# Where the split weights and the moving rows of a two-layer block lie in SBUF: one spacing for all slots, one place for all rows

## The chip, the cores and the metric

One Trainium2 chip, one core of it, fp32 in and out. The metric is the device time of one launch in microseconds (us), the median of several runs. Five engines run side by side: TensorE (PE; its weight loads are a row of their own, PEld), VectorE (DVE), ScalarE (ACT), GpSimd (POOL) and SyncE (SP).

## The reference

256 tokens of width 1024 go through two layers. Each layer is, with one shared shape of step `x = x + gate * f(modulate(rms_norm(x)))`:

```python
for l in range(2):
    mod = silu(c) @ w_ada[l] + b_ada[l]                      # 9 vectors of 1024
    x = x + 0.5 * g1 * swiglu(h1, w_ff_in[l, 0], w_ff_out[l, 0])    # 1024 -> 2 x 2816 -> 1024
    x = x + g2 * token_mix(h2, ...)                          # window attention, RG-LRU, gated linear attention
    x = x + 0.5 * g3 * swiglu(h3, w_ff_in[l, 1], w_ff_out[l, 1])

def token_mix(h, ...):
    proj = h @ w_in                                          # 1024 -> 6416
    ys = [attention(...), rg_lru(...), gla(...)]             # three branches of 1024
    merged = sum_b sigmoid(h @ w_gate_b) * (ys[b] @ w_branch_b)
    return merged @ w_out
```

Nearly all of the arithmetic is in products of the 256 tokens with fp32 weights that are read once.

## The kernel before

**Slabs.** All weights are cut into slabs of 128 partitions x 2048 fp32, 8192 bytes in each partition: eight blocks `cc` of 128 input rows by 256 output columns, or, for the output product of a feed-forward half (`slab_rows`), two blocks of 128 rows by 1024 columns. There are 120 slabs to a layer, numbered `p` in the order in which TensorE uses them. SyncE loads slab `p` into `raw` slot `p % 4`. ScalarE copies it, rounded to fp32r, into `w_hi` slot `p % 3` (line 964), and VectorE puts the rest, `raw - w_hi`, into `w_lo` slot `p % 3` (line 1438). The activations are split in the same way (`h_hi`, `h_lo` and so on).

**A product.** For a slab, TensorE runs 48 matmuls of 128 x 128 weights and 256 moving columns (`slab_tile`, line 490). They come in threes: weights `w_hi` with rows `hi`, `w_hi` with rows `lo`, `w_lo` with rows `hi`. While one matmul streams its moving rows, the weights of the next are loaded:

```python
for q, (a, b) in enumerate(((w[0], hi), (w[0], lo), (w[1], hi))):
    last = mm(outs, a, b[:, cc, :], ...)
```

214 of the 240 slabs go through line 490. The others: lines 514 and 520 (first slab after a norm), 534 (in chunks, as pieces arrive), 620 (the lead of a norm, 258 columns), 680 (16 columns) and 837 (the values of the linear attention, where rows of `h` are the weights and the slab moves).

**What moves.** `h_hi`/`h_lo` (8 rows of 256 floats) for the input, gate and output projections. In a feed-forward half, block `j` of the hidden layer lies in `hid_hi`/`hid_lo` for even `j` and in the first two rows of `xm_hi`/`xm_lo` for odd `j`. The branch products of the token mix read `y_hi`/`y_lo`, which are views of the same `xm_hi`/`xm_lo`. The rows of `xm` are 258 floats apart, since the lead of a norm multiplies 256 tokens and a doubled shift column.

**Order in a feed-forward half.** It is written out by hand: gate slab of `j + 1`, output slab of `j`, up slab of `j + 1`, and so on. With three slots the output slabs (`down`) nearly all fall into slot 0, and the up and gate slabs into slots 1 and 2. So six slabs repeat: even output (slot 0), up (slot 1), gate (slot 2), odd output (slot 0), up (slot 1), gate (slot 2).

**Where the tiles lie.** Tiles are taken one behind the other in the order of the `sb(...)` calls. Counted from the start of `raw`, in bytes of a partition: `w_hi` at 32768, its slots 8256 apart (2048 + 16 floats); `w_lo` at 57536, also 8256 apart; `h_hi` 100736, `h_lo` 108928; `xm_hi` 117120, `xm_lo` 125376, rows 1032 apart; `hid_hi` 133632, `hid_lo` 135680.

Of the kernel before, what the change touches and what calls it, by code (L numbers as in the profile page):

```python
# [8 lines left out]
F32R = mybir.dt.float32r  # L9
# [8 lines left out]
T = 256  # L18
C = D // P
# [17 lines left out]
SPLIT = 3  # L37
# [67 lines left out]
def build(nc, x, c, w_ada, b_ada, norm_g, w_ff_in, w_ff_out, w_in, qk_norm_g, attn_sinks, rel_bias,  # L105
# [3 lines left out]
    with ctx:  # L109
        def sb(name, shape, dt=F32):  # L110
            return ctx.enter_context(nc.sbuf_tensor(name, [P] + shape, dt))
# [3 lines left out]


        raw = sb("raw", [RAW, 2048])
        w_hi = sb("w_hi", [SPLIT, 2048 + 16], F32R)[:, :, 0:2048]
        w_lo = sb("w_lo", [SPLIT, 2048 + 16], F32R)[:, :, 0:2048]
        rgw = sb("rgw", [2, 2, P])  # L120

        xT = sb("xT", [C, T])
        hf = sb("hf", [C, T])
        h_hi, h_lo = sb("h_hi", [C, T], F32R), sb("h_lo", [C, T], F32R)
        xm_hi, xm_lo = sb("xm_hi", [C, T + 2], F32R), sb("xm_lo", [C, T + 2], F32R)
        y_hi, y_lo = xm_hi[:, :, 0:T], xm_lo[:, :, 0:T]
        hid_hi, hid_lo = sb("hid_hi", [2, T], F32R), sb("hid_lo", [2, T], F32R)
        hid_h = (hid_hi[:, :, :], y_hi[:, 0:2, :])
        hid_l = (hid_lo[:, :, :], y_lo[:, 0:2, :])
        merged = hf  # L130


# [1763 lines left out]
```

## Time and profile before

| | |
|---|---|
| three runs | 1554.15, 1557.41, 1557.48 us; median 1557.41 |
| profiled execution | 1556.63 us, its span in the profile 1554.9 us |
| TensorE matmuls / weight loads busy | 1530.3 us / 1486.8 us |
| VectorE busy | 1133.2 us |
| ScalarE busy | 801.3 us |
| DMA | 333.52 MB, mean 214 GB/s |
| mean granted TensorE clock | 0.993 of full |

The span is the time from the first to the last instruction of the program. Matmuls are pipelined: the profile gives each some 280 ns although the next one starts after about 118 ns, so what a matmul costs is read from start to start, or from a row of the chain that puts many matmuls of one line together, and not from the mean of one.

### The profile page before, as it was taken

Reading aid. Unit: us, or ns where it says so; the run is one execution under the profiler, and the core shown is the slowest. Engines: PE = TensorE matmul, PEld = TensorE weight load, DVE = VectorE, ACT = ScalarE, POOL = GpSimd, SP = SyncE. Lnnn points to the kernel's source line nnn. Section 1 sums busy time; section 2 is a strip of 40 time slices with the busy share of each in tenths; the row PEclk is TensorE's granted clock in tenths of the full one; section 3 lists DMA queues with packets and bytes.
Section 4 is the critical chain, followed back from the end, with each engine's and each line's share of the span. In section 5 each row is a group of like instructions: output and inputs, shape, how many; then the busy total and the mean of one; then the engine's idle time right before and its main releaser. Section 6 shows DMA issues by size and latency. Waiting matters only on the chain.

```text
span 1554.9 us, 29266 instructions
## 1 busy us (share of the span) xinstructions
PE 1530.3 (98%) x12591; PEld 1486.8 (96%) x12591; DVE 1133.2 (73%) x1533; ACT 801.3 (52%) x970; POOL 25.2 (2%) x29
## 2 busy tenths in 40 slices
PE   7999999999999999999999999999999999999998
PEld 6999999999999999999999999999999899999998
DVE  4597777898556998776877768769865588977444
ACT  3444337888446346433464334677855544463342
POOL 0000000000100000000000000000001000000000
PEclk8899999999999999999999999999999999999999
DMA  9889855554456886778658785555454599675451
GB/s 338 291 246 282 280 170 163 151 158 140 144 163 214 301 305 210 260 265 284 208 202 284 259 295 168 147 166 149 138 161 145 171 310 330 217 256 198 164 192 52
DMA packets 284001, 333.52 MB, mean 214 GB/s; under 512 B 13084, under 2 KB 235200, under 8 KB 283872
## 3 DMA queue, kind: packets, MB, share of 16 engines
q1 hardware_dynamic: 276112, 327.40, 64.1%
q10 hardware_dynamic: 7760, 4.26, 1.1%
q8 instruction: 99, 1.62, 0.4%
q14 instruction: 30, 0.25, 0.1%
HBM read 330.23 MB, written 1.38 MB: 213 GB/s over the span
## 4 chain that ended last, share of the span: by engine, by line
PE 84%; DVE 10%; ACT 4%; issue 1%; DMA 0%; SPq 0%; DVEq 0%; ACTq 0%
PE ps L490 71%; DVE w_lo L1438 3%; PE ps L837 3%; DVE scratch L1335 1%; ACT w_hi L964 1%; PE ps L752 1%; PE ps L552 1%; DVE hf L1482 1%; DVE h_lo L1487 1%; PE ps L620 1%; PE ps L698 1%; DVE xT L1502 1%; PE ps L553 1%; PE ps L799 1%; PE ps L514 1%
## 5 line engine op out<-in xcount | busy, mean ns | idle before, releaser
L490 PE MATMUL ps<-h_hi,w_hi 128*128 128x256 f32 x2336 | 659.9, 282 | 0.8 <-DVE w_lo L1438 0.8
L490 PE MATMUL ps<-h_lo,w_hi 128*128 128x256 f32 x2336 | 653.2, 280 | 0.0
L490 PE MATMUL ps<-h_hi,w_lo 128*128 128x256 f32 x2336 | 651.4, 279 | 0.0
L1438 DVE TENSOR_TENSOR w_lo<-raw,w_hi 128x2048 fp32r<-128x2048 f32 x237 | 541.1, 2285 | 120.7 <-ACT w_hi L964 120.7
L964 ACT ACTIVATE w_hi<-raw 128x2048 fp32r<-128x2048 f32 x237 | 452.6, 1913 | 207.8 <-PE ps L490 203.1
L490 PEld LDWEIGHTS ps<-h_hi,w_hi 128*128 128x128 f32 x2336 | 438.3, 188 | 8.9 <-issue 7.1
L490 PEld LDWEIGHTS ps<-h_lo,w_hi 128*128 128x128 f32 x2336 | 439.8, 188 | 0.5 <-issue 0.5
L490 PEld LDWEIGHTS ps<-h_hi,w_lo 128*128 128x128 f32 x2336 | 439.8, 188 | 0.0
L490 PE MATMUL ps<-xm_hi,w_hi 128*128 128x256 f32 x704 | 199.8, 284 | 0.0
L490 PE MATMUL ps<-xm_hi,w_lo 128*128 128x256 f32 x704 | 198.7, 282 | 0.0
L490 PE MATMUL ps<-xm_lo,w_hi 128*128 128x256 f32 x704 | 197.9, 281 | 0.0
L1335 DVE SCALAR_TENSOR_TENSOR scratch<-eyr,cond,scratch 128x512 f32<-128x512 f32 x240 | 180.3, 751 | 10.5 <-DMA eyr<-in_w_ada_dram 1.7
L1551 DVE TENSOR_TENSOR t512b<-t512a,ps 128x512 f32<-128x512 f32 x41 | 28.2, 687 | 144.5 <-issue 92.9
L490 PEld LDWEIGHTS ps<-xm_hi,w_lo 128*128 128x128 f32 x704 | 133.1, 189 | 0.0
L490 PEld LDWEIGHTS ps<-xm_lo,w_hi 128*128 128x128 f32 x704 | 133.1, 189 | 0.0
L490 PEld LDWEIGHTS ps<-xm_hi,w_hi 128*128 128x128 f32 x704 | 132.9, 189 | 0.0
L490 PE MATMUL ps<-hid_hi,w_hi 128*128 128x256 f32 x384 | 109.1, 284 | 1.4 <-DVE hid_lo L1555 1.3
L490 PE MATMUL ps<-hid_lo,w_hi 128*128 128x256 f32 x384 | 108.1, 282 | 0.0
L490 PE MATMUL ps<-hid_hi,w_lo 128*128 128x256 f32 x384 | 107.1, 279 | 0.0
L490 PEld LDWEIGHTS ps<-hid_hi,w_hi 128*128 128x128 f32 x384 | 72.1, 188 | 2.0 <-DVE w_lo L1438 1.6
L490 PEld LDWEIGHTS ps<-hid_hi,w_lo 128*128 128x128 f32 x384 | 73.0, 190 | 0.0
L490 PEld LDWEIGHTS ps<-hid_lo,w_hi 128*128 128x128 f32 x384 | 72.2, 188 | 0.1
(269 smaller groups left out, 1762.8 us busy)
## 6 DMA issues: line engine op xcount, KB each, us to landing
raw<-in_w_ff_in_dram SPq DMA_DIRECT2D x176, 512.0 KB, 4.8
eyr<-in_w_ada_dram SPq DMA_DIRECT2D x144, 512.0 KB, 6.9
raw<-in_w_in_dram SPq DMA_DIRECT2D x100, 512.0 KB, 4.7
raw<-in_w_ff_out_dram SPq DMA_DIRECT2D x88, 512.0 KB, 4.8
raw<-in_w_gate_dram SPq DMA_DIRECT2D x48, 512.0 KB, 4.6
raw<-in_w_branch_dram SPq DMA_DIRECT2D x48, 512.0 KB, 4.6
raw<-in_w_out_dram SPq DMA_DIRECT2D x16, 512.0 KB, 5.3
rgw<-in_rg_w_dram ACTq DMA_DIRECT2D x16, 128.0 KB, 2.2
```

Of the source, the lines that this page charges most:

```text
L490: last = mm(outs, a, b[:, cc, :], start=clear and cc == 0 and q == 0, stop=cc == n - 1 and q == 2, skip_group_check=True)
L514: mm(ps[:, bank, t * T:(t + 1) * T], w_of[b][:, cc, t * P:(t + 1) * P], h_hi[:, cc, :], start=cc == 0 and b == 0 and t == 0, stop=False, s ...
L552: mm(to, ada_raw(2 * b + 1)[:, cc, cols], cond[:, 4 + cc:5 + cc], start=cc == 0, stop=False)
L553: last = mm(to, acc[:, cols], ones[:, 0:1], start=not direct, stop=True)
L620: last = mm(ps[:, first_bank + t, 0:T + 2], a, b[:, cc, :], start=cc == 0 and q == 0, stop=cc == C - 1 and q == 2, skip_group_check=True)
L698: last = nc.tensor.transpose(ps[:, 4 + hh, b * P:(b + 1) * P], pr[:, hh, b * P:(b + 1) * P], ident[:, :])
L752: last = mm(ps[:, 2 - g, t * T:(t + 1) * T], rgw[:, g, t, :], xc[:, t, :], start=True, stop=True)
L837: last = mm(ps[:, 1, m * T:(m + 1) * T], a, b, start=cc == 0 and q == 0, stop=cc == C - 1 and q == 2)
L964: f(w_hi[:, p % SPLIT, :], raw[:, p % RAW, :], ACT.Copy).then_inc(hi_ready, 1)
L1335: ins = stt(acc, w[:, cc, :], by, acc, ALU.mult, ALU.add)
L1438: tt(w_lo[:, p % SPLIT, :], raw[:, p % RAW, :], w_hi[:, p % SPLIT, :].bitcast(F32), ALU.subtract).then_inc(lo_ready, 1)
L1551: tt(t512b[:, :], t512a[:, :], ps[:, 5, :], ALU.mult).then_inc(hid_made, 1)
```

## The change

The split weights lose the pad of 16 floats behind each slot, so that slots lie exactly 8192 bytes apart. A pad of 192 bytes is put between `w_hi` and `w_lo`, and one of 128 bytes ahead of `h_hi`. `xm_hi` and `xm_lo` become two halves of one flat tile `xm`; the branch rows `y_hi`, `y_lo` become a view of it of their own, with rows 1024 bytes apart (not 1032) and `y_lo` 8192 bytes behind `y_hi`. The odd hidden block still lies in the first two rows of `xm_hi`/`xm_lo`, 1032 bytes apart, and `hid_hi`/`hid_lo` move ahead of `xm`. No instruction is added or removed.

```diff
-        w_hi = sb("w_hi", [SPLIT, 2048 + 16], F32R)[:, :, 0:2048]
-        w_lo = sb("w_lo", [SPLIT, 2048 + 16], F32R)[:, :, 0:2048]
+        w_hi = sb("w_hi", [SPLIT, 2048], F32R)
+        sb("place_low", [48])
+        w_lo = sb("w_lo", [SPLIT, 2048], F32R)
         rgw = sb("rgw", [2, 2, P])
 
         xT = sb("xT", [C, T])
         hf = sb("hf", [C, T])
+        sb("place_h", [32])
         h_hi, h_lo = sb("h_hi", [C, T], F32R), sb("h_lo", [C, T], F32R)
-        xm_hi, xm_lo = sb("xm_hi", [C, T + 2], F32R), sb("xm_lo", [C, T + 2], F32R)
-        y_hi, y_lo = xm_hi[:, :, 0:T], xm_lo[:, :, 0:T]
         hid_hi, hid_lo = sb("hid_hi", [2, T], F32R), sb("hid_lo", [2, T], F32R)
-        hid_h = (hid_hi[:, :, :], y_hi[:, 0:2, :])
-        hid_l = (hid_lo[:, :, :], y_lo[:, 0:2, :])
+        xm = sb("xm", [2 * C * (T + 2)], F32R)
+        xm_hi, xm_lo = (xm[:, b * C * (T + 2):(b + 1) * C * (T + 2)].rearrange("p (c t) -> p c t", c=C) for b in range(2))
+        y_hi, y_lo = (xm[:, b * C * T:(b + 1) * C * T].rearrange("p (c t) -> p c t", c=C) for b in range(2))
+        hid_h = (hid_hi[:, :, :], xm_hi[:, 0:2, 0:T])
+        hid_l = (hid_lo[:, :, :], xm_lo[:, 0:2, 0:T])
```

## Rows read from the trace of the kernel before

**Rows 1.** The page: busy time of each engine, its share of the span, instructions.

```profile
PE 1530.3 (98%) x12591; PEld 1486.8 (96%) x12591; DVE 1133.2 (73%) x1533; ACT 801.3 (52%) x970; POOL 25.2 (2%) x29
```

**Rows 2.** Busy time by stretch: us, PE, PEld, DVE, ACT, POOL; granted clock, DMA, GB/s.

```profile
250.00:378.00 128.00, 127.30 (x1045) 119.41 (x1044) 108.49 (x219) 104.46 (x181) 0.00 (x0) 1.00 0.51 151
...
626.00:798.00 172.00, 170.93 (x1448) 170.64 (x1449) 127.42 (x134) 70.11 (x56) 0.00 (x0) 1.00 0.76 256
```

**Rows 3.** The chain that ended last: start, length, what, how many.

```profile
54.25 146.93 PE ps L490 x1248
...
625.98 135.65 PE ps L490 x1152
818.03 135.65 PE ps L490 x1152
...
1378.51 135.65 PE ps L490 x1152
```

**Rows 4.** The same chain between 240 and 600 us, shares by line.

```profile
by line: PE ps L490 60.7%; PE ps L837 6.5%; DVE w_lo L1438 4.0%; issue 2.2%; PE ps L752 2.0%; DVE scratch L1335 1.9%; ACT w_hi L964 1.6%; PE ps L698 1.5%; PE ps L799 1.3%; PE ps L795 1.2%; PE ps L865 1.2%; PE ps L741 1.1%; DVE hf L1482 0.9%
```

**Rows 5.** Timeline, a feed-forward half: first matmul of seven slabs in a row.

```profile
65.60 0.28 PE L490 MATMUL ps<-hid_hi,w_hi 128*128 128x256 f32 x1
...
71.26 0.28 PE L490 MATMUL ps<-h_hi,w_hi 128*128 128x256 f32 x1
...
76.80 0.28 PE L490 MATMUL ps<-h_hi,w_hi 128*128 128x256 f32 x1
...
82.45 0.28 PE L490 MATMUL ps<-xm_hi,w_hi 128*128 128x256 f32 x1
...
88.15 0.28 PE L490 MATMUL ps<-h_hi,w_hi 128*128 128x256 f32 x1
...
93.80 0.28 PE L490 MATMUL ps<-h_hi,w_hi 128*128 128x256 f32 x1
...
99.46 0.28 PE L490 MATMUL ps<-hid_hi,w_hi 128*128 128x256 f32 x1
```

**Rows 6.** Timeline, first and last matmul of two slot 0 slabs of `h`.

```profile
346.54 0.27 PE L490 MATMUL ps<-h_hi,w_hi 128*128 128x256 f32 x1
...
352.06 0.28 PE L490 MATMUL ps<-h_hi,w_lo 128*128 128x256 f32 x1
...
549.71 0.28 PE L490 MATMUL ps<-h_hi,w_hi 128*128 128x256 f32 x1
...
555.29 0.28 PE L490 MATMUL ps<-h_hi,w_lo 128*128 128x256 f32 x1
```

**Rows 7.** Timeline, first and last matmul of a branch slab, slot 1.

```profile
501.61 0.28 PE L490 MATMUL ps<-xm_hi,w_hi 128*128 128x256 f32 x1
...
507.24 0.28 PE L490 MATMUL ps<-xm_hi,w_lo 128*128 128x256 f32 x1
```

**Rows 8.** Timeline, after a pause: second and last matmul of three slabs.

```profile
256.24 0.28 PE L490 MATMUL ps<-h_lo,w_hi 128*128 128x256 f32 x1
...
261.76 0.28 PE L490 MATMUL ps<-h_hi,w_lo 128*128 128x256 f32 x1
...
333.42 0.28 PE L490 MATMUL ps<-h_lo,w_hi 128*128 128x256 f32 x1
...
338.84 0.28 PE L490 MATMUL ps<-h_hi,w_lo 128*128 128x256 f32 x1
...
538.62 0.28 PE L490 MATMUL ps<-h_lo,w_hi 128*128 128x256 f32 x1
...
543.94 0.27 PE L490 MATMUL ps<-h_hi,w_lo 128*128 128x256 f32 x1
```

**Rows 9.** Line 1438, the low halves: duration ns min/median/max, first and last start.

```profile
L1438 DVE TENSOR_TENSOR w_lo<-raw,w_hi x237: 2260/2284/2295, 51.8 to 1533.7; 128x2048 fp32r<-128x2048 f32 x119
```

**Rows 10.** Line 964, the high halves: the same.

```profile
L964 ACT ACTIVATE w_hi<-raw x237: 1896/1912/1943, 37.2 to 1531.8; 128x2048 fp32r<-128x2048 f32 x119
```

**Rows 11.** Waits of TensorE on the low halves: us in total, times, longest.

```profile
PE ps L490 <- DVE w_lo L1438: 0.8, 2, 0.4
```

## The prediction

> **What bounds the kernel now.** I read the page first, then the chain of waits, then stretches, then single matmuls. TensorE is busy for 1530 of 1554.9 us, VectorE for 73% and ScalarE for 52% of the span [rows 1]. In a feed-forward half TensorE fills 170.93 of 172 us while VectorE has 127 [rows 2]; there the chain that ends last is nothing but matmuls of line 490, 1152 of them in 135.65 us, three times, and 1248 in 146.93 us [rows 3]. That is 117.75 ns from one matmul to the next. In the token mix VectorE and ScalarE are busier (108 and 104 of 128 us [rows 2]), but line 490 still holds 60.7% of the chain between 240 and 600 us, 218.5 us [rows 4]; the 43 slabs of that line in the stretch need about 43 x 5.65 = 243 us, so 90% of them lie on the chain. TensorE waited for a low half of the weights for 0.8 us in all [rows 11]. So what a matmul takes from start to start decides, and the change, which adds and removes no instruction, can act only through that.
>
> **What the trace says about places.** The reader is to see in [rows 5] that slabs with the same work do not take the same time. Per slab of 48, from first matmul to first matmul: even output (slot 0) 5.66 us; up (slot 1) 5.54; gate (slot 2) 5.65; odd output (slot 0) 5.70; up (slot 1) 5.65; gate (slot 2) 5.66. So 115.5 ns a matmul at best and 118.75 at worst, without a pause. It repeats: the chain's 117.75 ns is the mean of this six, 33.86 us for 288 matmuls, 117.6 ns, with a few edges. Slot 0 of `h` took (352.06 - 346.54) / 47 = 117.4 ns once and 118.7 ns another time [rows 6]; a branch slab 119.8 ns [rows 7]; the first one after a pause, slot 0 of `h`, 5.52 / 46 = 120.0 ns [rows 8].
>
> What differs is where the moving rows lie to the weights. From the sizes of the tiles, byte places modulo 512 (one weight tile is 512 bytes of a partition), rows `hi` minus `w_hi`, then rows `lo` minus `w_lo`: `h` with slot 0: 384, 192; slot 1: 320, 128; slot 2: 256, 64. Even hidden block with slot 0: 0, 320. Odd: 384 or 392, 256 or 264. Branch rows in slot 1: 320 to 376, 192 to 248, moving by 8 with each row. The only pair that reaches 115.5 ns is `h` with slot 1: 320 and 128.
>
> After the change `w_hi` is at 0, `w_lo` at 192 and `h`, `hid` and `y` all at 320 for `hi` and `lo`, in every slot. That is 320, 128 everywhere; the distances of `h` from the weights equal those of slot 1 before even modulo 8192. Only the odd hidden block differs (320 or 328, 192 or 200), with the leads of line 620, whose rows stay 1032 bytes apart.
>
> **But the place does not decide alone.** The two up slabs of [rows 5] have the same places, and the one behind an odd output took 5.65 us, not 5.54. After a pause one slab at this place went at 5.42 / 46 = 117.8 ns and another at 5.32 / 46 = 115.7 ns [rows 8]. So 320, 128 carries two rhythms, and how it is entered picks one; each then held to the end of its slab. In the feed-forward halves the entry from an even output always gave the fast one and that from an odd output always the slow one; of 17 entries after a pause or other work, by my count, 14 gave the fast one. With one place everywhere there is nothing at a slab's edge to change a rhythm, and the fast one should run on until an odd output.
>
> **The sum, if the fast rhythm holds.** Feed-forward halves: line 490 has 122 slabs there, 20 of them odd outputs; of the other 102, 20 are already fast. 82 x (5.65 - 5.54) = 9.0 us. Odd outputs: no row has their new pair at length. The nearest from below is 115.5 ns (same place for `hi`), the nearest from above the branch slab's 119.8 ns, whose first two rows have just these distances; against 118.75 now that is -3.1 to +1.0 us for 20 slabs. I take 0, nearer to the upper row. Token mix, both layers: 24 slabs of `h` in slot 2, 0.11 us each, 2.6 us; 24 in slot 0, between 117.4 and 118.7, mean 118.05, less 115.5, 0.12 us each, 2.9 us; 24 branch slabs, 119.8 to 115.5, 0.20 us each, 4.8 us; 4 slabs in chunks (line 534), slot 2, 0.4 us; the 20 in slot 1 stay. 10.7 us. From it comes the entry: most of these slabs begin after a pause, where slabs at this place need some matmuls to fall into step, or miss it (3 of 17). I estimate 2 us. Of the 8.7 left 90% are on the chain: 7.8 us. Lines 620 and 837 keep the kind of distance that they have: 0.
>
> The edits that cost nothing: VectorE's copies of line 1438 took 2260 to 2295 ns and ScalarE's of line 964 1896 to 1943 ns [rows 9, 10], over slots that lie 0, 64 and 128 bytes off `raw`'s place modulo 512; all will lie at 0 or 192, and 0 is among those measured for reading. The flat view changes no count of elements. If these copies became slower by 0.1 us each, VectorE's 45 us of slack in 172 [rows 2] would hide it in the halves; 28 slabs or so in the first part of each mix would pay, under 6 us.
>
> Together 9.0 + 7.8 = 16.8 us, against an execution of 1556.63 us whose span is 1554.9; that execution lies 0.8 us under the median of 1557.41, within the runs' spread of 3.3. From the median: 1540.6; I say 1541 us.
>
> **Rivals.** (A) As above. Chance 0.48, own range 1535 to 1545.
>
> (B) The odd output throws the rhythm out, as it does now, and since nothing after it differs any more, the slow rhythm runs on to the next pause: 117.7 ns for all of the half except some 30 slabs, against 20 fast ones now. 10 x 0.11 = 1.1 us instead of 9.0, and the mix as before: 8.9 us, 1548.5 us. For it: the slow rhythm also held to the slab's end each time. Against: the new odd output keeps `hi` at 320 in its first row, and most entries fall fast. Chance 0.26.
>
> (C) Nothing. The difference between slabs comes from what TensorE did before, not from addresses, or losses and gains cancel. For it: equal places gave unequal times. Against: three slots give three steady times in the same sequence. All at 117.7 ns would be 214 slabs at the mean they have: about 1556 us. Chance 0.16.
> By the Trainium skill ("SBUF — State Buffer", section "Who interferes with whom") TensorE has two independent read ports, one for moving rows and one for weight loads, and never waits on anyone. By that rule no placement can matter and the sum is 0; this trace does not agree with it as it stands, since slabs of equal work took 5.54 and 5.70 us.
>
> (D) Slower: equal spacing of all slots takes away the 64 bytes that kept the slot being written apart from the one being read, modulo 512; with one place for all, ScalarE's and VectorE's writes beat against TensorE's reads, and the rhythm settles at the 120.0 ns of [rows 8]. 214 x 48 x (120.0 - 117.75) = 23.1 us: 1580 us. It decides from a mean of line 490 over 117.8 ns. Against it: fast and slow slabs keep their times exactly while copies start and stop. Chance 0.10.
>
> **How the numbers follow.** A and B give a time more than 0.2% (3.1 us, about what a measurement of this kernel can tell from no change) below the median, and part of C does: faster 0.79. Same 0.12, slower 0.09. The low end takes A with the odd outputs at 115.5 ns and no loss at entries: 16.8 + 3.1 + 2 = 21.9, 1535 us. The high end reaches past B to 1553 us; what is left above is most of C and D, 0.2.
>
> **What would show it.** Right: the long pieces of the chain shrink from 135.65 us for 1152 matmuls to about 133.6 (A) or 135.3 (B); after an even output, an up and a gate slab and the output take 5.54 us each; branch slabs drop from 5.63 to about 5.43 us over 47 intervals; copies keep their 2284 and 1912 ns. Wrong: slot 1 slabs lose their 5.54 us (the place was not the cause), or all three slots agree on 5.65 us or more (B, C, D), or the time saved on TensorE comes back as waits on line 1438.

## The result and the profile after

The changed kernel took 1544.33 us, the median of 4 runs from 1542.41 to 1547.53, against 1555.78 for the kernel before beside it (4 runs, 1553.84 to 1557.48). The ratio is 0.9927, with a 95% interval of 0.9914 to 0.994. I had said 1541 us, 1535 to 1553. The profiled execution took 1546.22 us, with a span of 1544.4: 10.5 us less span where the prediction's sum had 16.8.

The page, engine by engine (busy us, share of the span, instructions), to be read beside [rows 1]:

```profile
PE 1516.1 (98%) x12591; PEld 1472.5 (95%) x12591; DVE 1133.3 (73%) x1533; ACT 801.2 (52%) x970; POOL 25.2 (2%) x29
```

The same instructions on each engine; only TensorE is busy for less, by 14.2 us. VectorE and ScalarE keep their busy time to 0.1 us. So does each copy, in the lines' durations (ns, min/median/max), which answer to [rows 9, 10]:

```profile
L1441 DVE TENSOR_TENSOR w_lo<-raw,w_hi x237: 2267/2285/2295, 52.2 to 1523.3; 128x2048 fp32r<-128x2048 f32 x119
```

```profile
L967 ACT ACTIVATE w_hi<-raw x237: 1896/1912/1946, 39.0 to 1521.4; 128x2048 fp32r<-128x2048 f32 x119
```

The chain that ended last (start, length, what), to be read beside [rows 3]:

```profile
54.79 145.86 PE ps L493 x1248
...
622.48 134.31 PE ps L493 x1152
813.21 134.61 PE ps L493 x1152
...
1369.68 134.31 PE ps L493 x1152
```

The prediction gave 133.6 for its case A and 135.3 for B. 134.31 is 116.6 ns a matmul, against 117.75 before: nearer to A, and short of it. The timeline of seven slabs in a row, first matmuls, shows why; it answers to [rows 5]:

```profile
133.45 0.28 PE L493 MATMUL ps<-hid_hi,w_hi 128*128 128x256 f32 x1
...
139.00 0.28 PE L493 MATMUL ps<-h_hi,w_hi 128*128 128x256 f32 x1
...
144.55 0.28 PE L493 MATMUL ps<-h_hi,w_hi 128*128 128x256 f32 x1
...
150.09 0.28 PE L493 MATMUL ps<-xm,w_hi 128*128 128x256 f32 x1
...
155.84 0.29 PE L493 MATMUL ps<-h_hi,w_hi 128*128 128x256 f32 x1
...
161.42 0.28 PE L493 MATMUL ps<-h_hi,w_hi 128*128 128x256 f32 x1
...
166.97 0.28 PE L493 MATMUL ps<-hid_hi,w_hi 128*128 128x256 f32 x1
```

Even output 5.55 us, up 5.55, gate 5.54, then the odd output 5.75, and behind it up 5.58 and gate 5.55. The fast rhythm now holds in all three slots and comes back within one slab of an odd output; the odd output itself went from 5.70 to 5.75 us. The fast rhythm isn't always entered, though. An `h` slab near the start of the first half, before any odd output, took 5.66 us in the same places:

```profile
71.58 0.28 PE L493 MATMUL ps<-h_hi,w_hi 128*128 128x256 f32 x1
...
77.24 0.28 PE L493 MATMUL ps<-h_hi,w_hi 128*128 128x256 f32 x1
```

A branch slab, first and last matmul, beside [rows 7]: 5.43 us over 47 intervals instead of 5.63.

```profile
498.95 0.28 PE L493 MATMUL ps<-xm,w_hi 128*128 128x256 f32 x1
...
504.38 0.27 PE L493 MATMUL ps<-xm,w_lo 128*128 128x256 f32 x1
```

Last, TensorE's waits (us in total, times, longest), first of before, then of after. The six kinds of wait on ScalarE and VectorE in the second list grew by 1.0, 0.1, 1.2, 0.4, 0.6 and 0.2 us, 3.5 us together ([rows 11] has the old one on the low halves). Of the others, a wait on a DMA grew by 0.2 and the longest one, at the start, fell from 7.3 to 6.9:

```profile
PE ps L567 <- DVE mod L1359: 3.2, 3, 1.1
PE ps L607 <- ACT hf L988: 2.8, 4, 1.2
...
PE ps L490 <- DVE hid_lo L1555: 1.3, 2, 0.6
...
PE ps L534 <- DVE h_lo L1815: 0.7, 2, 0.4
```

```profile
PE ps L570 <- DVE mod L1362: 4.2, 3, 1.4
PE ps L610 <- ACT hf L991: 2.9, 4, 1.4
...
PE ps L537 <- DVE h_lo L1818: 1.9, 2, 1.0
PE ps L493 <- DVE hid_lo L1558: 1.7, 3, 0.8
PE ps L744 <- ACT t512a L1156: 1.2, 4, 0.4
PE ps L493 <- DVE w_lo L1441: 1.0, 2, 0.5
```

(The wait that became 1.2 us stood at 0.6 before, on line 741.) TensorE comes to these points earlier, while what it waits for there comes no earlier by as much.

I worked the rest out by laying the 214 slabs of the two traces beside each other, start and end of each. In the table, "within" is what was saved between the first and last matmuls of the slabs, "between" what was taken back outside them (gaps from one slab to the next, head and tail of the kernel), in us:

```
part                       predicted   within   between    net
feed-forward halves (4)        9.0       6.1      -1.6     4.5
token mix (both layers)        7.8       8.5      -2.5     6.0
together                      16.8      14.6      -4.1    10.5
```

### The profile page after: what moved, and what is told of

Read it like the earlier page. It is cut to its first block, busy times and chain, and to the rows that moved or that the text cites. A ratio compares the mean times of both kernels' runs of the same rounds, so it can differ in the third digit from the quotient of the medians.

```text
span 1544.4 us, 29266 instructions
## 1 busy us (share of the span) xinstructions
PE 1516.1 (98%) x12591; PEld 1472.5 (95%) x12591; DVE 1133.3 (73%) x1533; ACT 801.2 (52%) x970; POOL 25.2 (2%) x29
## 4 chain that ended last, share of the span: by engine, by line
PE 79%; DVE 11%; ACT 6%; issue 2%; DMA 0%; SPq 0%; DVEq 0%; ACTq 0%
PE ps L493 67%; DVE w_lo L1441 4%; PE ps L840 3%; ACT w_hi L967 2%; DVE scratch L1338 2%; PE ps L555 1%; DVE hf L1485 1%; DVE h_lo L1490 1%; PE ps L755 1%; DVE xT L1505 1%; ACT L980 1%; PE ps L556 1%; ACT xm L993 1%; PE ps L701 1%; PE ps L802 1%
## 5 line engine op out<-in xcount | busy, mean ns | idle before, releaser
L1441 DVE TENSOR_TENSOR w_lo<-raw,w_hi 128x2048 fp32r<-128x2048 f32 x237 | 541.3, 2286 | 118.0 <-ACT w_hi L967 117.9
L493 PE MATMUL ps<-xm,w_hi 128*128 128x256 f32 x1408 | 251.0, 281 | 0.0
L493 PEld LDWEIGHTS ps<-xm,w_hi 128*128 128x128 f32 x1408 | 215.1, 189 | 0.0
L493 PE MATMUL ps<-xm,w_lo 128*128 128x256 f32 x704 | 197.0, 280 | 0.0
L493 PEld LDWEIGHTS ps<-xm,w_lo 128*128 128x128 f32 x704 | 132.7, 189 | 0.0
L1036 ACT ACTIVATE t512a<-ps 128x512 f32<-128x512 f32 x41 | 24.5, 598 | 85.8 <-PE ps L493 83.5
L1059 ACT ACTIVATE xm<-t512b 128x512 fp32r<-128x512 f32 x20 | 12.7, 635 | 88.8 <-DVE t512b L1554 88.8
```

The lines of the kernel that those rows point to most:

```text
L493: last = mm(outs, a, b[:, cc, :], start=clear and cc == 0 and q == 0, stop=cc == n - 1 and q == 2, skip_group_check=True)
L1036: f(t512a[:, :], ps[:, 4, :], ACT.Silu).then_inc(silu_ready, 1)
L1441: tt(w_lo[:, p % SPLIT, :], raw[:, p % RAW, :], w_hi[:, p % SPLIT, :].bitcast(F32), ALU.subtract).then_inc(lo_ready, 1)
```

## The experiments

One theory is the prediction's: the places of the moving rows to the weights, taken modulo some power of two, set the time of a matmul, and the time before them picks among a few rhythms. Its rivals: the slot or the order of work sets it, not the place (prediction's C), or the distance to what VectorE and ScalarE write does (D). Every kernel of this section is compared with the kernel before, which took 1554.10 to 1556.86 us on the chips of these runs (medians, the lowest a single run). "ns a matmul" is always from start to start, without pauses. A "rhythm" is such an interval that holds from matmul to matmul; "64, 128" as a pair means rows `hi` 64 bytes past `w_hi` and rows `lo` 128 bytes past `w_lo`.

### TensorE alone, at 80 sets of places

A kernel that computes nothing of the reference and has only these matmuls, in bursts of 96 with a pause between: 64 pairs of places, then 8 places of `w_lo` with 320, 128 kept, then all four areas moved together.

```diff
+    out = [(0, LOW, dh, LOW + dl) for dh in range(0, 512, 64) for dl in range(0, 512, 64)]
+    out += [(0, wl, 320, wl + 128) for wl in range(0, 512, 64)]
+    out += [(a, a + LOW, a + 320, a + LOW + 128) for a in range(0, 512, 64)]
...
+                for r in range(2):
+                    for t in range(2):
+                        for cc in range(8):
+                            w = [v[:, cc, t * P:(t + 1) * P] for v in (w_hi, w_lo)]
+                            for q, (a, b) in enumerate(((w[0], hi), (w[0], lo), (w[1], hi))):
```

> A kernel of TensorE alone, nothing of the reference is computed: 80 bursts of 96 matmuls in the threes of line 490, after a pause each, with no copies and no DMA beside them. 64 bursts take rows hi minus w_hi and rows lo minus w_lo through 0, 64, ... 448 bytes modulo 512; 8 keep 320 and 128 and move w_lo against w_hi; 8 keep 320 and 128 and move all four tiles together by 0, 64, ... 448. Theory 'place between moving rows and the weights being loaded': 320, 128 settles at 115.6 ns a matmul; 384, 192 and 256, 64 at 117.5 to 120; the last 16 bursts all at 115.6 or 117.7 (the two rhythms). Rival 'absolute place': the last 8 bursts differ among themselves. Rival 'copies of ScalarE and VectorE cause the stalls': all 80 bursts are alike.

The last 48 intervals of two bursts in the timeline, for the pairs 0, 0 and 320, 128:

```profile
18.50 0.28 PE L69 MATMUL ps<-m_hi,w_lo 128*128 128x256 f32 x1
...
24.26 0.28 PE L69 MATMUL ps<-m_hi,w_lo 128*128 128x256 f32 x1
...
534.02 0.28 PE L69 MATMUL ps<-m_hi,w_lo 128*128 128x256 f32 x1
...
539.57 0.27 PE L69 MATMUL ps<-m_hi,w_lo 128*128 128x256 f32 x1
```

5.76 / 48 = 120.0 ns and 5.55 / 48 = 115.6 ns, with nothing else running. All 64 pairs, each worked out in this way (down: `hi` minus `w_hi` in bytes; across: `lo` minus `w_lo`):

```
       0    64   128   192
  0  120.0 117.7 117.8 117.7
 64  115.5 117.8 115.6 117.8
128  120.0 117.5 117.8 117.8
192  117.8 117.8 120.0 119.2
```

From 256 on, down as across, the values come again to 0.4 ns: the period is 256 bytes, so 320, 128 is 64, 128. This agrees with the kernel before where its rows lie at one place: 0, 64 (gate slabs and even outputs) has 117.7 here and 117.7 to 117.9 there. The odd output doesn't fit as well: 128, 0 has 120.0 here, and 118.7 there, with its second row 8 bytes further on. Moving all four areas together left 115.6 ns at all eight places; moving `w_lo` alone gave 116.7 or 117.8, although the place behind one of these 117.8 is the very one that the first series has at 115.6. So the place decides, without slots, copies or DMA (against C and D). It doesn't decide alone: one pair can have two rhythms.

### Everything 64 bytes further, and everything at distance 0

The first moves all that the change places, to see whether it is the distance to the weights or the address (or the distance to `raw`) that matters. The second keeps the equal spacing and the flat rows and takes both pads out, so that `w_lo` and the rows lie at 0 modulo 512 to the weights.

```diff
         raw = sb("raw", [RAW, 2048])
+        sb("place_all", [16])
         w_hi = sb("w_hi", [SPLIT, 2048], F32R)
```

```diff
         w_hi = sb("w_hi", [SPLIT, 2048], F32R)
-        sb("place_low", [48])
         w_lo = sb("w_lo", [SPLIT, 2048], F32R)
...
-        sb("place_h", [32])
         h_hi, h_lo = sb("h_hi", [C, T], F32R), sb("h_lo", [C, T], F32R)
```

> The changed kernel with 64 bytes more between raw and w_hi, so that weights and moving rows move together, away from raw. Theory 'place between rows and weights': no change, slabs of h and y at 115.6 ns, odd outputs at 119.7, span within 3 us of 1544. Rival 'absolute place of the slots' or 'place of w_hi to raw': the slabs go back to 117.7 or more, span 1555 or above.

> The changed kernel without either pad: slots 8192 apart, all moving rows and w_lo at place 0 to w_hi. Theory 'place between rows and weights, 320 and 128 is good': the mean of the slabs of line 490 is not 115.6 but 117.7 or above, span 1550 to 1585. Rival 'equal spacing of the slots is what helps, whichever the place': 115.6 ns, span 1544.

The chain of the first, then of the second:

```profile
622.74 134.32 PE ps L494 x1152
```

```profile
631.39 138.02 PE ps L491 x1152
```

With everything 64 bytes further, one run took 1546.15 us and had a span of 1544.4, the same as after, and the same 115.6 and 119.7 ns in its slabs. At distance 0 one run took 1572.87 us, 16 us slower than the kernel before: 138.02 / 1152 = 119.8 ns. That is close to the table's 120.0 for 0, 0, although `w_lo` lay 192 bytes past `w_hi` there and at the same place here. Equal places alone gain nothing. The pads do it, by where they put the rows.

### The flat view alone, and the change without it

`flat_alone` is the kernel before with the branch rows packed; `no_flat_rows` is the kernel after with the branch rows 1032 bytes apart again. The flat view changes two things at once: the distance from row to row, and the place of `y_lo`, which moves by 64 bytes to the weights (192 to 128). What each is worth wasn't run by itself.

```diff
-        xm_hi, xm_lo = sb("xm_hi", [C, T + 2], F32R), sb("xm_lo", [C, T + 2], F32R)
-        y_hi, y_lo = xm_hi[:, :, 0:T], xm_lo[:, :, 0:T]
+        xm = sb("xm", [2 * C * (T + 2)], F32R)
...
+        y_hi, y_lo = (xm[:, b * C * T:(b + 1) * C * T].rearrange("p (c t) -> p c t", c=C) for b in range(2))
```

```diff
-        y_hi, y_lo = (xm[:, b * C * T:(b + 1) * C * T].rearrange("p (c t) -> p c t", c=C) for b in range(2))
+        y_hi, y_lo = xm_hi[:, :, 0:T], xm_lo[:, :, 0:T]
```

> The kernel before with the flat view of xm alone: slots 8256 bytes apart, h and y at 384, 192 to slot 0, 320, 128 to slot 1, 256, 64 to slot 2. Theory 'place': branch slabs in slot 1 at 115.6 ns, in slots 0 and 2 at 117.5 to 120 as h; h slabs and odd outputs as before; 1554 us. Rival 'the flat view is the whole gain': 1544.

> The changed kernel with the branch rows back at 1032 bytes apart (320 + 8 cc, 192 + 8 cc to the weights). Theory 'place': the 24 branch slabs go from 115.6 back to about 119.8 ns, 4.8 us more; all else stays: 1549 us when its rhythms are those of the changed kernel. Rival 'the flat view does nothing': 1544.

`flat_alone` took 1552.86 us (one run) and left the long pieces of the chain alone:

```profile
622.90 135.66 PE ps L491 x1152
```

Its branch slabs went from 119.9, 119.3 and 118.8 ns (slots 1, 0 and 2) to 116.0, 118.2 and 117.8: 2.6 us for the 24, pauses left out. `no_flat_rows` took 1548.23 us (one run); a branch slab in its chain:

```profile
500.00 5.75 PE ps L493 x48
```

5.75 / 48 = 119.8 ns, where the packed rows have 115.6. 24 such slabs x 48 x 4.2 ns = 4.8 us, the prediction's term for the branch rows; between their first and last matmuls, with the pauses in them, it was 4.5. The span grew by 2.1 us only over after's 1544.4: the heads of the first and the third half and some slabs behind pauses fell into the fast rhythm this time, which gave 1.4 us back, and the other 1.0 came off the gaps.

### The odd hidden block at the common place too

The odd block gets rows of its own, at the same places as `h`, in memory shared with two small tiles that are dead then; the load of the linear attention's gate weights into one of them is issued four slabs later. If the theory holds, the 5.75 us of an odd output become 5.55.

```diff
-        rgw = sb("rgw", [2, 2, P])
+        sb("place_h", [32])
+        with nc.sbuf_tensor("rgw", [P, 2, 2, P], F32) as rgw, nc.sbuf_tensor("kk", [P, 2, T], F32) as kk:
+            pass
+        odd_hi, odd_lo = sb("odd_hi", [2, T], F32R), sb("odd_lo", [2, T], F32R)
...
-        hid_h = (hid_hi[:, :, :], xm_hi[:, 0:2, 0:T])
+        hid_h = (hid_hi[:, :, :], odd_hi[:, :, :])
```

> The changed kernel with the odd hidden block at the common place too: it lies over rgw and kk (idle in the feed-forward halves) 1024 bytes apart in a row, the pad of 128 bytes stands ahead of them, and the load of gla_wg comes after four more slabs. Theory 'place', the fast rhythm kept: 20 slabs go from 119.7 to 115.6 ns (4.0 us) and the slabs behind them from 116.2 to 115.6 (0.6 us): ratio to the kernel before 0.990, 1540 us. With 'a slow rhythm runs on until something disturbs it', the odd output no longer ends it: halves that start slow (now slabs 1 to 5 of the first) stay at 117.7 to the next pause, which costs 2.5 us each; 1540 to 1546 us. Rival 'the odd output is slow for another reason': no gain.

It took 1543.33 us, the median of 6 runs; ratio to before 0.9918 [0.99, 0.9936], which can't be told from after's 0.9927. But its runs lie between 1539.20 and 1549.76, 10.6 us apart, where after's are 5.1 apart. The profiled one is the slowest, and its chain shows what happened:

```profile
55.42 144.69 PE ps L495 x1248
...
621.71 135.92 PE ps L495 x1152
813.93 135.92 PE ps L495 x1152
1371.26 135.92 PE ps L495 x1152
```

The first half ran at 115.6 ns, odd outputs among it, and is 1.2 us shorter than after's. The other three ran at 135.92 / 1152 = 118.0 ns from the first matmul to the last. Nothing differs between these halves in places. The entry fell into the slow rhythm, and with no place changing anywhere, nothing ended it for 24 slabs and more. The odd output of the changed kernel, slow itself, looks like what brings the fast rhythm back; the next two runs try that.

### An odd place left in on purpose, once and twice in each half

If that is so, one or two odd outputs at the other place, early in each half, should make the rest fast whatever the entry.

```diff
-        hid_h = (hid_hi[:, :, :], odd_hi[:, :, :])
+        hid_h = (hid_hi[:, :, :], odd_hi[:, :, :], xm_hi[:, 0:2, 0:T])
...
-                        f(hid_h[j % 2], t512b[:, :].rearrange("p (a t) -> p a t", a=2), ACT.Copy).then_inc(hid_hi_ready, 1)
+                        f(hid_h[2 if j == 1 else j % 2], t512b[:, :].rearrange("p (a t) -> p a t", a=2), ACT.Copy).then_inc(hid_hi_ready, 1)
```

(The same for the low half and for the matmuls; twice: `j in (1, 3)`.)

> As odd_too, but the first odd block (j = 1) of each feed-forward half stays in the rows of xm, at the place where the rhythm of the changed kernel always came out fast; the other 16 odd outputs are at the common place. Theory 'a slow rhythm runs on until something disturbs it': all slabs behind the first odd output run at 115.6 ns in every execution; 16 odd outputs save 4.1 ns x 48 each, 3.1 us, against the changed kernel; 1540 us, and the runs lie closer together than the 10.6 us of odd_too. Rival 'the slow halves of odd_too have another cause (the place over rgw and kk)': halves at 117.8 ns appear here too, 1540 to 1549 us.

> As odd_reset, but with j = 1 and j = 3 in the rows of xm, so that the pause in front of slab 11 in the first half, after which odd_reset ran slow, has a disturbing block behind it. Theory 'a slow rhythm runs on until something disturbs it': slabs 19 to 26 at 115.6 ns always, 1 us more for the second block in each half is 0.8 us in all; 1541 us, lowest to highest under 5 us. Rival 'the odd rows of xm do not end the slow rhythm, chance does': slow halves as before, 1543 us and up.

Once: 1543.27 us, median of 6 runs from 1539.17 to 1544.64, ratio 0.9909 [0.9896, 0.9922]. The chain:

```profile
54.32 146.63 PE ps L495 x1248
622.70 133.62 PE ps L495 x1152
812.75 133.91 PE ps L495 x1152
1368.28 133.59 PE ps L495 x1152
```

Three halves have the 133.6 us of the prediction's case A. The first has not: after its one odd output it ran fast up to slab 11, whose first interval is 195 ns, some 0.08 us longer than the others, and went on at 117.8 ns to its end, which the expectation, fast behind the first odd output in every execution, had ruled out. The changed kernel, the one before this and the one after it have the same short pause at that slab (193 to 194 ns; the kernel before has none), and all three went on at 115.6 ns. So a pause of under a tenth of a microsecond can change the rhythm, and doesn't do so always: the slow halves of `odd_too` kept theirs over such a pause, 0.09 us longer than an interval.

Twice: 1542.83 us, median of 5 runs, ratio 0.9916 [0.9902, 0.993]. In the profile the four halves were fast but for six slabs at the seams of the second and the fourth, and the runs lie between 1542.18 and 1543.64, 1.5 us apart. In the profiles each slab behind an odd output at the other place, and without a pause of its own, ended at 115.5 to 115.6 ns: 17 of 17 in the changed kernel, 4 of 4 and 8 of 8 here, slow slabs ahead of the odd output or not. So the odd output does bring the fast rhythm back. The three medians can't be told apart. The spread of the runs falls, 10.6, 5.5 and 1.5 us over 6, 6 and 5 runs on three chips. That the returns are what narrows it is likely and not shown: the changed kernel, with five returns in each half, spreads over 5.1 us in 4 runs.

### All pairs in steps of 16 bytes

`map_fine` has the 256 pairs of a period of 256 in bursts of 48, and then 64, 0 and 64, 128 in turn. `map_repeat` has each pair four times in mixed order, behind pauses of seven lengths. Neither computes anything of the reference.

```diff
-    out = [(0, LOW, dh, LOW + dl) for dh in range(0, 256, 16) for dl in range(0, 256, 16)]
-    out += [(0, LOW, 64, LOW + dl) for n in range(12) for dl in (0, 128)]
+    out = []
+    for rep in range(4):
+        for n in np.random.default_rng(rep).permutation(256):
+            dh, dl = 16 * (int(n) // 16), 16 * (int(n) % 16)
+            out.append((0, LOW, dh, LOW + dl))
```

> TensorE alone as in the first map, bursts of 48, distances of both pairs in steps of 16 bytes over 256, and then 12 bursts each at 64, 0 and 64, 128. Theory 'a stall each time that two streams meet in the same part of 256 bytes': a band of good places some 32 to 64 bytes wide around 64, and nothing under 115.5 ns. Rival 'fixed points only': good values at multiples of 64 alone. The last 24 bursts: mostly 115.6, some 117.8 ns if the rhythm is chance; all the same if the place decides.

> TensorE alone again, each of the 256 pairs of distances (steps of 16 bytes) four times in a mixed order, with pauses of seven lengths. Theory 'the pair sets which rhythms exist, the entry picks one': 64, 0 and 64, 128 give both 115.5 and 117.8 ns, 16, 240 gives 113.3 ns at least once in four, and most other pairs never fall under 115. Rival 'the pair decides alone': all four bursts of a pair agree. If 16, 240 gives 113.3 ns all four times it is the place for a faster kernel: 2.2 ns less on 10272 matmuls would be 23 us.

The commonest interval is 117.8 ns, in 454 of the 1024 bursts of the second, before 118.9 (115) and 120.0 (77); the mean is 118.08. Of the 256 pairs 167 gave the same within 0.3 ns in all four bursts, so the rival that the pair decides alone fell for the rest. Both theories written down for `map_fine` missed: good places form no band, and something lies under 115.5 ns. In `map_fine` one pair was faster than all I had seen, `hi` 16 bytes and `lo` 240 bytes past their weights. `map_repeat` gave it in all four of its bursts; 24 intervals of one of them:

```profile
1489.52 0.28 PE L71 MATMUL ps<-m_hi,w_lo 128*128 128x256 f32 x1
...
1492.24 0.28 PE L71 MATMUL ps<-m_hi,w_lo 128*128 128x256 f32 x1
```

2.72 / 24 = 113.3 ns. Means of the last 24 intervals of each of the four bursts of some pairs in `map_repeat`:

```
 16, 240   113.3 four times
 64,   0   115.5 to 115.6 four times (also 16, 128; 64, 112; 112, 0)
 64, 128   117.8 117.8 115.6 115.5   (the place of the change)
  0,   0   120.0 four times
```

So the change's pair is one of those with two rhythms, as the trace of before had hinted. How often each comes depends on what goes before: 115.6 ns in 12 of its 13 bursts of the first experiment, in 2 of 4 here, and in 6 of the 12 that end `map_fine`. Those bursts, with 64, 0 in turn, took 117.8 ns in every other burst of either pair. So 64, 0 has two rhythms as well, though `map_repeat` shows one. Three pairs, (16, 128), (64, 112) and (112, 0), took 115.5 to 115.6 in all five of their bursts in both maps, and (16, 240) took 113.3.

### All rows at 16, 240

The whole kernel with `h`, both hidden blocks and the branch rows 16 bytes past `w_hi` and 240 past `w_lo`. The high rows are cut out of one area behind `w_hi`, the low rows out of one behind `w_lo`, each with a short lead.

```diff
         w_hi = sb("w_hi", [SPLIT, 2048], F32R)
-        sb("place_low", [48])
...
+        his = sb("his", [4 + 12 * T + 44], F32R)
         w_lo = sb("w_lo", [SPLIT, 2048], F32R)
...
+        los = sb("los", [60 + 12 * T + 2 * C * (T + 2) + 4], F32R)
...
+        odd_hi, h_hi, hid_hi = rows(his, 4, 2), rows(his, 4 + 2 * T, C), rows(his, 4 + 10 * T, 2)
+        odd_lo, h_lo, hid_lo = rows(los, 60, 2), rows(los, 60 + 2 * T, C), rows(los, 60 + 10 * T, 2)
...
+        y_lo, y_hi = rows(xm, 0, C), rows(xm, C * T + 24, C)
```

> The whole kernel with every moving row of line 490, the odd block too, at the best pair of the maps: rows hi 16 bytes past w_hi and rows lo 240 past w_lo, modulo 512. Theory 'the place between rows and weights sets the rhythm, whatever the other engines do': slabs at 113.3 ns in each half of each execution, with no second rhythm; 4.5 ns less than before on 10272 matmuls is 46 us of matmul time, of which the changed kernel's own record (15.6 us less on matmuls, 10.5 us less in span) lets about two thirds through: 1520 to 1530 us. Rival 'the maps do not carry over, since copies and DMA run beside the matmuls here': 115.6 to 118 ns, 1540 to 1555.

It took 1523.20 us, the median of 4 runs from 1521.50 to 1526.58, against 1556.32 for before beside it: ratio 0.9793 [0.9778, 0.9807]. It is faster than both kernels. Chain, timeline and waits:

```profile
612.22 130.81 PE ps L499 x1152
800.69 130.81 PE ps L499 x1152
1349.36 130.82 PE ps L499 x1152
```

```profile
128.45 0.28 PE L499 MATMUL ps<-his,w_hi 128*128 128x256 f32 x1
```

```profile
PE ps L576 <- DVE mod L1368: 5.2, 3, 1.8
PE ps L616 <- ACT hf L997: 3.6, 4, 1.6
PE ps L499 <- DVE w_lo L1447: 2.4, 4, 0.8
```

130.81 / 1152 = 113.6 ns. The first matmuls of the slabs that follow the one shown lie at 133.89, 139.33 and 144.77 us, 5.44 apart each, in all slots. Between the first and last matmuls of the 214 slabs it saves 41.4 us against before (some 45 by their intervals with pauses left out, where the change of this document has some 16), and the span fell by 35.1, to 1519.8: 85% of the 41.4. The waits have grown again, line 499's on the low halves from 0.8 us [rows 11] to 2.4.

One wait did more. Ahead of the slab at 761.62 us TensorE had stood idle for the 1.8 us of line 576's longest wait (before: 1.1, after: 1.4). From 762.28 to 765.68 us its granted clock was 0.50, the 1.2 GHz level, and 16 matmuls in a row were 212 to 214 ns apart, 1.6 us lost. In before and after the granted clock stays 1.00 there. That the longer wait is the reason is not shown: it happened once in this trace.

The expectation of one rhythm held: without such an event or a pause in it, every slab ended at 113.3 ns. Its 4 runs still lie 5.1 us apart, so rhythms are not all that makes runs differ.

## Why the prediction was right, and by how much it was off

**What bounds the kernel.** Right. No instruction was added or removed, only the distance from matmul to matmul changed, and the time followed it, in both directions: 1572.87, 1555.78, 1544.33 and 1523.20 us at 119.8, 117.75, 116.6 and 113.6 ns in the long pieces of the chain.

**That the place decides.** Right, and shown three ways: by TensorE alone, by the shift of everything (no effect) and by the distance 0 (slower). The prediction read places modulo 512; the values come again after 256.

**The time.** 1544.33 us is 3.3 off, and part of that closeness is luck. The sum gave 16.8 us less and 11.45 were measured; the median of before, 1557.41 in the three runs that the prediction had, came to 1555.78 with a fourth.

**That the fast rhythm runs on (A) or the slow one (B).** Both, by what follows. The changed kernel behaves as A: the slab behind an odd output took 5.58 us, the next 5.55. But its slow rhythm did last in slabs 1 to 5 and in 123 to 125, to the next odd output each time. The prediction took the odd output for what spoils the rhythm; here it restored it each time. Where it was taken out, the slow rhythm ran through three whole halves, which is B, without its cause.

**Feed-forward term, 82 x 0.11 = 9.0 us.** Mis-sized: 6.1 us within slabs, 4.5 net. A slab at 117.8 that goes to 115.6 saves 48 x 2.2 ns = 0.105 us, not 0.11 (-0.4). The slabs behind the 20 odd outputs lose 0.03 us of that each (-0.6). Eight slabs at the heads of the first and the third half were slow, six that should have gained and two that had been fast before (-0.8). With the odd outputs of the next term (-1.0) that makes 6.2. And gaps took back 1.6.

**Odd outputs, 0 within -3.1 to +1.0.** Mis-sized, at its upper end: 118.7 to 119.7 ns, 20 x 48 x 1.0 = 1.0 us more. I had noted that the branch slab's 119.8 ns [rows 7] was the row with just these distances and still took a value below it. The nearest row was the right price.

**Token mix, 10.7 less 2, 90% of it.** Close for the slabs: 8.5 us within against 8.7. The branch slabs came to 115.6 ns as said, but saved 4.1 us between first and last matmuls and not 4.8: not all had stood at 119.8, six of the 24 ended at 118.3 or 118.8 before. The factor of 90% was too mild: the gaps returned 2.5 us, and 6.0 were left where 7.8 were expected. It also rests on a count that was off: 45 slabs of line 490 start between 240 and 600 us, not 43, and 45 x 5.65 is 254 us, of which the chain's 218.5 are 86%. The chain had shown what share of this work lies on it, [rows 4], but not how near the next wait was. With TensorE faster, line 493's share of the chain between 240 and 600 us fell from 60.7% to 51.9%:

```profile
by line: PE ps L493 51.9%; PE ps L840 6.5%; issue 4.2%; DVE w_lo L1441 4.0%; DVE scratch L1338 3.4%; ACT w_hi L967 2.6%; PE ps L755 2.0%; PE ps L701 1.5%; PE ps L802 1.3%; PE ps L798 1.2%; PE ps L868 1.2%; PE ps L744 1.1%; ACT L980 1.1%; AC
```

**Nothing for the edits on the copies.** Right: 2285 and 1912 ns, as before.

**Rival C.** Fallen: the same distances without anything else running gave 115.6, 117.8 and 120.0 ns. The Trainium skill ("SBUF — State Buffer", section "Who interferes with whom") gives TensorE two independent read ports, one for moving rows and one for weight loads. By that rule no place of one to the other could matter; the runs speak against it here, with 113.3 to 120.0 ns in TensorE alone.

**Rival D.** Its time nearly came, 1572.87 us at distance 0 for everything, but not by its mechanism. TensorE alone shows the 120.0 ns of that pair (with `w_lo` at 192) with no engine writing. And the 64 bytes between slots that D wanted kept are absent in the fastest kernel as well.

**What stays open.** Why the period is 256 bytes, and what in the reads makes 16, 240 the best pair. Which rhythm a pause picks: the runs show only that it can pick, and that the pick lasts. How the distance of `w_lo` from `w_hi` enters: eight places are all that was tried. The extent to which single runs of one kernel differ by the rhythm they fell into (before: 1554 or 1557) was seen in the spread, not in traces of both, and 16, 240 spreads by 5.1 us with one rhythm. Whether 1032 bytes from row to row cost by themselves, or the place of `y_lo` that goes with them.

## What to carry to other kernels

Where matmuls of equal work take unequal times without a wait, measure the interval per slab and set it beside the places of both operands modulo a small power of two; a kernel of TensorE alone maps all pairs in two milliseconds, and the best pair here was worth 2.1%, where the change that was tried first gave 0.7%. Take a pair that gave the same time in every burst of every map over one that gave its best in half of them, since a rhythm once entered lasts until the place changes or the engine pauses. And of time saved on the engine that is the bound, expect back only some 70 to 85% (10.5 of 14.6 us, 35.1 of 41.4): waits that were just hidden come out, and one of them came with a lower clock.

## What the runs showed of the hardware

- Loading 128x128 fp32r weights for each matmul of 256 columns, TensorE settles in over half of the bursts at one of a few intervals: 113.3, 115.5, 117.8 or 120.0 ns, steps of 2.2 ns, at a mean granted clock of 1.00 in the kernels of TensorE alone, its 2.4 GHz level. Which one depends on the moving rows' places to the weights modulo 256 bytes; some pairs have two of them.
- In a pair with two, the one entered held for 24 slabs and more (over 130 us) without a pause, and a pause of 0.08 us changed it in one of the kernels that had it at the same slab.
- The worst pair of the 256 in the fine map, `hi` at 0 and `lo` at 32, took 122.2 ns, 8% more than the best.
- `w_lo` moved against `w_hi`, with each row's distance to its own weights kept, gave 117.8 ns at six of eight places, where the entry may have decided, and 116.7 at two, 256 bytes apart, in an even alternation of 348 and 352 ns for three matmuls. So a third distance may have a say too.
- In the kernel at 16, 240 the granted clock was 0.50 for 3.4 us, right after a wait of 1.8 us; 16 matmuls came 212 to 214 ns apart instead of 113.3.
